# A triangular solve by chunk in two 64x64 blocks per head, in one core's hybrid decoder layer

## The reference, cut to what matters

```python
decay = jnp.exp(jnp.where(tri, gam[..., :, None] - gam[..., None, :], -jnp.inf))
kb = kc * bc[..., None]
M = jnp.tril(jnp.einsum('nbhrd,nbhsd->nbhrs', kb, kc) * decay, -1)
A = M + jnp.eye(L, dtype=M.dtype)
rhs = jnp.concatenate([vc * bc[..., None], kb * jnp.exp(gam)[..., None]], axis=-1)
X = lax.linalg.triangular_solve(A, rhs, left_side=True, lower=True, unit_diagonal=True)
U, W = X[..., :dv], X[..., dv:]
```

## Time and profile before

| | us |
|---|---|
| median of 3 runs (lowest, highest) | 1853.58 (1852.49, 1855.44) |
| the profiled execution | 1853.64 |
| its span, from the first to the last instruction | 1851.8 |
| PE busy | 1829.1 (99%) |
| PEld busy | 1582.3 (85%) |
| DVE busy | 1065.3 (58%) |
| ACT busy | 855.7 (46%) |
| POOL busy | 452.2 (24%) |

### The profile page before, as it was taken

How to read it: one execution, slowest core, us unless ns; L and a number is a source line. 1 busy time by engine, 2 the same in 40 slices (tenths; PEclk the granted TensorE clock), 3 DMA queues, 4 the chain that set the end, 5 groups by cost and what they waited for, 6 DMA issues and landing times.

```text
span 1851.8 us, 26888 instructions
## 1 busy us (share of the span) xinstructions
PE 1829.1 (99%) x10213; PEld 1582.3 (85%) x10213; DVE 1065.3 (58%) x1267; ACT 855.7 (46%) x1004; POOL 452.2 (24%) x242
## 2 busy tenths in 40 slices
PE   8999999999999999999999999999999999999997
PEld 6888988888888888888888878888888888888886
DVE  5677743455655675555555356666666666543334
ACT  5555445435643344444444354444444444444444
POOL 5222533112231122222222232222222222222223
PEclk9999999999999999999999999999999999999999
DMA  7566443444444456656667636665566566655553
GB/s 209 168 182 192 138 126 125 121 130 137 159 157 128 137 184 196 189 182 189 191 187 248 200 130 193 192 189 186 182 192 188 185 192 188 211 193 192 193 193 135
DMA packets 263432, 324.50 MB, mean 175 GB/s; under 512 B 16779, under 2 KB 230213, under 8 KB 262725
## 3 DMA queue, kind: packets, MB, share of 16 engines
q1 hardware_dynamic: 263366, 323.58, 55.3%
HBM read 321.45 MB, written 2.10 MB: 175 GB/s over the span
## 4 chain that ended last, share of the span: by engine, by line
PE 96%; DVE 2%; ACT 1%; issue 0%; DMA 0%; DVEq 0%; SPq 0%; ACTq 0%
PE ps L571 94%; PE ps L652 0%; DVE xs L1799 0%; PE ps L722 0%; DMA x_in<-in_x_dram 0%; ACT p L992 0%; DVE w_lo L380 0%; PE ps L683 0%; PE ps L870 0%; ACT w_hi L375 0%; ACT L992 0%; PE ps L847 0%; DVE gvt L1667 0%; DVE p L1434 0%; DVE fmax L1439 0%
## 5 line engine op out<-in xcount | busy, mean ns | idle before, releaser
L375 ACT ACTIVATE w_hi<-raw 128x1024 fp32r<-128x1024 f32 x601 | 635.0, 1059 | 872.5 <-PE ps L571 861.2
L380 DVE TENSOR_TENSOR w_lo<-raw,w_hi 128x1024 fp32r<-128x1024 f32 x450 | 561.9, 1255 | 504.1 <-ACT w_hi L375 503.4
L571 PE MATMUL ps<-xnT,w_hi 128*128 128x512 f32 (+1 forms) x2960 | 750.2, 395 | 0.9 <-issue 0.8
L380 POOL TENSOR_TENSOR w_lo<-raw,w_hi 128x1024 fp32r<-128x1024 f32 x151 | 368.2, 2438 | 1307.8 <-ACT w_hi L375 1307.7
L571 PEld LDWEIGHTS ps<-xnT,w_hi 128*128 128x128 f32 (+1 forms) x2960 | 532.4, 189 | 99.1 <-issue 1.5
L571 PEld LDWEIGHTS ps<-xnT,w_lo 128*128 128x128 f32 (+1 forms) x2960 | 404.2, 190 | 29.3
L571 PE MATMUL ps<-xnT,w_lo 128*128 128x256 f32 (+1 forms) x2960 | 415.4, 282 | 0.0
L571 PE MATMUL ps<-w_hi,xnT 128*128 128x512 f32 x1408 | 356.6, 392 | 0.0
L571 PEld LDWEIGHTS ps<-w_hi,xnT 128*128 128x128 f32 x1408 | 261.3, 188 | 52.8 <-issue 0.2
L571 PE MATMUL ps<-w_lo,xnT 128*128 128x512 f32 x704 | 192.4, 390 | 1.6 <-DVE w_lo L380 1.6
L571 PEld LDWEIGHTS ps<-w_lo,xnT 128*128 128x128 f32 x704 | 132.0, 188 | 29.8 <-DVE w_lo L380 2.3
(11 more groups left out here) (330 smaller groups left out, 1089.7 us busy)
## 6 DMA issues: line engine op xcount, KB each, us to landing
raw<-in_w_in_dram SPq DMA_DIRECT2D x256, 512.0 KB, 3.6
raw<-in_w_up_dram SPq DMA_DIRECT2D x176, 512.0 KB, 3.6
raw<-in_w_down_dram SPq DMA_DIRECT2D x88, 512.0 KB, 4.6
raw<-in_w_out_dram SPq DMA_DIRECT2D x32, 512.0 KB, 4.7
raw<-in_w_fox_proj_dram SPq DMA_DIRECT2D x16, 512.0 KB, 4.1
raw<-in_w_gdn_proj_dram SPq DMA_DIRECT2D x16, 512.0 KB, 3.2
raw<-in_w_ml_proj_dram SPq DMA_DIRECT2D x16, 512.0 KB, 3.8
x_in<-in_x_dram SPq DMA_DIRECT2D x4, 512.0 KB, 5.7
```

The source lines that it names most:

```text
L375: act.activation(w_hi[:, s, 0:n], raw[:, s, 0:n], ACT.Copy).then_inc(hi_ready[s], 1)
L380: eng.tensor_tensor(w_lo[:, s, 0:n], raw[:, s, 0:n], w_hi[:, s, 0:n], ALU.subtract).then_inc(lo_ready[s], 1)
L571: return pe.matmul(o, l, r, start=start, stop=stop)
```

## The change

Both chunks of a tile are now kept one above the other, as blocks of 64 columns: nt_, nlv, xm and xmt become [128, NT, H, 64], with chunk 0 in partitions 0 to 63 and chunk 1 in 64 to 127. Each product of 128x128 becomes two of 64x64, one with rows and columns 0 to 63 of the array and one with 64 to 127, issued in turn for each head. The two write different partitions of the same bank.

- **plan_items**: all items of both tiles for one step share a slot, and steps are two slots apart. Steps: solve_p 0, solve_p 1, then for levels 1 to 5 solve_x and solve_p; 24 items in 12 slots, 64, 66 to 86. wt is at 88 instead of 96. What follows moves 8 slots earlier, from dc on 6. mturn gets a bound on the chunks of mlqk, and dc one more slot behind mlv, with a wait for each.
- **solve_p** of level lv > 0 first transposes xm (16 products with the identity, into the pair's second bank) and then, but for the last (6), multiplies nlv by xm (16, into the first bank). Level 0 multiplies nlv by the identity. ACT copies the transpose to xmt; DVE scales the product by c_m into the new tile xp, at level 0 also forms xm, and then waits for ACT's copy (xt_turned) before it frees the pair. solve_xt is gone.
- **solve_x** (levels 1 to 5): xmt times xp, 16 products; DVE subtracts it from xm.
- **wt** and **u**: 16 products instead of 8, each of one block; wt writes a bank for each block.
- **DVE** forms nt_ in two operations of 64 partitions; its block of six operations (kbg, gvt, gkt) comes behind solve_p of level 5.
- **POOL**: masks of 128x512 instead of 128x1024; the two triangular selects on nt_ (L1936) are gone, one addition folds the level masks, one makes ident_c.

```diff
+    out += [(at, "solve_p", (tt, 0)) for tt in range(NT)]
+    at += 2
     for lv in range(LEVELS):
-        row = [("solve_p", 0), ("solve_p", 1)]
-        row += [("solve_x", 0), ("solve_x", 1)] * (0 < lv < LEVELS - 1)
-        row += [("solve_xt", 0), ("solve_xt", 1)]
-        for name, tt in row:
-            out.append((at, name, (tt, lv)))
-            at += 1
+        for name in ("solve_x",) * (0 < lv < LEVELS) + ("solve_p",):
+            out += [(at, name, (tt, lv + (name == "solve_p"))) for tt in range(NT)]
+            at += 2
...
-    out.append((gx, "mturn", ()))
+    out.append((max(gx, last_chunk("mlqk", 3) + 2), "mturn", ()))
...
-    at = max(at, last_chunk("mlv", 1)) + 1
+    at = max(at, last_chunk("mlv", 1) + 1) + 1
...
+        BLOCKS = (slice(0, L), slice(L, P))
+
+        def within(ap, b):
+
+            return ap[:, b, :].rearrange("p (h l) -> p h l", l=L)
...
                 elif name == "solve_p":
                     tt, lv = args
-                    pe.wait_ge(S["level_ready"], 2 * lv + tt + 1)
+                    if lv < LEVELS:
+                        pe.wait_ge(S["level_ready"], 2 * lv + tt + 1)
...
-                    for h in range(H):
-                        if lv:
-                            last = mm(oh[:, h, :], nlv[:, tt, h, :], xm[:, tt, h, :])
-                        else:
-                            last = pe.transpose(oh[:, h, :], nlv[:, tt, h, :], ident[:, :])
+                    for h in range(H * (lv > 0)):
+                        for r in BLOCKS:
+                            last = mm(within(o, 1)[r, h, :], xm[r, tt, h, :], ident[r, r])
+                    for h in range(H * (lv < LEVELS)):
+                        for r in BLOCKS:
+                            last = mm(within(o, 0)[r, h, :], nlv[r, tt, h, :], xm[r, tt, h, :] if lv else ident[r, r])
                 elif name == "solve_x":
                     tt, lv = args
                     item_read(pe, "solve_p", tt, lv)
...
+                        for r in BLOCKS:
+                            last = mm(within(o, 0)[r, h, :], xmt[r, tt, h, :], xp[r, tt, h, :])
...
-                        last = mm(oh[:, h, :], kbg[:, tt, h, :], xmt[:, tt, h, :])
...
+                        for cb, r in enumerate(BLOCKS):
+                            last = mm(within(o, cb)[:, h, :], kbg[r, tt, h, :], xmt[r, tt, h, :])
...
-                        last = mm(oh[:, h, :], xmt[:, tt, h, :], gvt[:, tt, h, :])
...
+                        for r in BLOCKS:
+                            last = mm(oh[r, h, :], xmt[r, tt, h, :], gvt[r, tt, h, :])
...
-                    for h in range(H):
-                        last = f(pm_[:, tt, h, :], heads(o)[:, h, :], ACT.Identity, scale=c_m[:, tt, h:h + 1], bias=0.0)
-                    last.then_inc(free, 1)
...
+                    f(xmt[:, tt, :, :], within(o, 1), ACT.Copy).then_inc(S["xt_turned"] if lv < LEVELS else free, 1)
...
+                    tt_(xp[:, tt, :, :], within(o, 0), over_free(c_m[:, tt, :], L), ALU.mult).then_inc(S["xp_ready"], 1)
+                    dve.wait_ge(S["xp_ready"], 2 * lv + tt + 1)
+                    if lv == 0:
+                        dve.wait_ge(S["ident_ready"], 1)
+                        tt_(xm[:, tt, :, :], over_heads(ident_c[:, :], H), xp[:, tt, :, :],
                             ALU.subtract).then_inc(S["x_start"], 1)
+                    else:
+                        dve.wait_ge(S["xt_turned"], 2 * (lv - 1) + tt + 1)
+                    dve.sem_inc(free, 1)
+                elif name == "solve_x":
+                    tt, lv = args
+                    item_written(dve, k)
+                    if lv == 1:
+                        dve.wait_ge(S["x_start"], tt + 1)
+                    tt_(xm[:, tt, :, :], xm[:, tt, :, :], within(o, 0), ALU.subtract).then_inc(free, 1)
```

More of the change, by code:

```diff
@@ L245, in hybrid_layer_kernel @@
         start_b = small("start_b", [P, NT])
+        ident_c = small("ident_c", [P, L])
         arena = cursor[0] + (-cursor[0]) % 1024
@@ L266, in hybrid_layer_kernel @@
         aqk = part("aqk", 8, [P, NT, H, P])
-        nt_ = part("nt", 10, [P, NT, H, P])
-        xm = part("xm", 12, [P, NT, H, P])
-        xmt = part("xmt", 14, [P, NT, H, P])
+        nt_ = part("nt", 10, [P, NT, H, L])
+        xmt = part("xmt", 14, [P, NT, H, L])
         pm_ = part("pm", 16, [P, NT, H, P])
+        xp = part("xp", 16, [P, NT, H, L])
+        xm = part("xm", 17, [P, NT, H, L])
         ed = part("ed", 18, [P, NT, H, P])
         sq = part("sq", 18, [P, NT, H, HD])
-        nlv = part("nlv", 18, [P, NT, H, P])
+        nlv = part("nlv", 18, [P, NT, H, L])
         st = part("st", 10, [P, H, HD])
@@ L707, in item @@
                     item_read(pe, "solve_p", tt, lv)
-                    if lv:
-                        item_read(pe, "solve_xt", tt, lv - 1)
                     for h in range(H):
[L711 to L717, removed]
-                    for h in range(H):
[L719 to L722, removed]
+                        for r in BLOCKS:
+                            last = mm(within(o, 0)[r, h, :], xmt[r, tt, h, :], xp[r, tt, h, :])
                 elif name == "wt":
@@ L725, in item @@
                     pe.wait_ge(S["kbg_ready"], tt + 1)
-                    item_read(pe, "solve_xt", tt, LEVELS - 1)
+                    item_read(pe, "solve_p", tt, LEVELS)
                     for h in range(H):
-                        last = mm(oh[:, h, :], kbg[:, tt, h, :], xmt[:, tt, h, :])
+                        for cb, r in enumerate(BLOCKS):
+                            last = mm(within(o, cb)[:, h, :], kbg[r, tt, h, :], xmt[r, tt, h, :])
                 elif name == "u":
@@ L1036, in item @@
                     f(ed[:, tt, :, :], ed[:, tt, :, :], ACT.Exp).then_inc(S["e_exp"], 1)
-                elif name == "solve_p":
+                elif name == "solve_p" and args[1] > 0:
                     tt, lv = args
                     item_written(act, k)
[L1040 to L1043, removed]
-                        last = f(pm_[:, tt, h, :], heads(o)[:, h, :], ACT.Identity, scale=c_m[:, tt, h:h + 1], bias=0.0)
-                    last.then_inc(free, 1)
-                elif name == "solve_xt" and 0 < args[1] < LEVELS - 1:
-                    item_written(act, k)
-                    f(xmt[:, args[0], :, :], heads(o), ACT.Copy).then_inc(free, 1)
+                    f(xmt[:, tt, :, :], within(o, 1), ACT.Copy).then_inc(S["xt_turned"] if lv < LEVELS else free, 1)
                 elif name == "wt":
@@ L1051, in item @@
                     item_written(act, k)
-                    f(wq[:, tt, :, 0:4:3, :], heads(o).rearrange("p h (b l) -> p h b l", l=L), ACT.Copy,
+                    f(wq[:, tt, :, 0:4:3, :], o.rearrange("p b (h l) -> p h b l", l=L), ACT.Copy,
                       scale=-1.0).then_inc(free, 1)
@@ L1370, in item @@
                     dve.wait_ge(S["dk_ready"], tt + 1)
-                    tt_(nt_[:, tt, :, :], oh, ed[:, tt, :, :], ALU.mult).then_inc(free, 1)
+                    for r in BLOCKS:
+                        last = tt_(nt_[r, tt, :, :], oh[r, :, r], ed[r, tt, :, r], ALU.mult)
+                    last.then_inc(free, 1)
                 elif name == "qk":
@@ L1381, in item @@
                     tt_(q_t, q_t, pm_[:, tt, :, :], ALU.mult).then_inc(S["qg_ready"], 1)
-                elif name == "solve_x" or name == "solve_xt" and args[1] in (0, LEVELS - 1):
+                elif name == "solve_p" and args[1] < LEVELS:
                     tt, lv = args
                     item_written(dve, k)
-                    m = (xm if name == "solve_x" else xmt)[:, tt, :, :]
-                    tt_(m, m if lv else over_heads(ident[:, :], H), oh, ALU.subtract).then_inc(free, 1)
                     if lv == 0:
-                        tt_(xm[:, tt, :, :], over_heads(ident[:, :], H), pm_[:, tt, :, :],
-                            ALU.subtract).then_inc(S["x_start"], 1)
+                        dve.wait_ge(S["qg_ready"], 2)
+                        dve.wait_ge(S["coef_ready"], 1)
+                    tt_(xp[:, tt, :, :], within(o, 0), over_free(c_m[:, tt, :], L), ALU.mult).then_inc(S["xp_ready"], 1)
[3 more added lines that the diff above has]
+                        tt_(xm[:, tt, :, :], over_heads(ident_c[:, :], H), xp[:, tt, :, :],
+                            ALU.subtract).then_inc(S["x_start"], 1)
+                    else:
[7 more added lines that the diff above has]
+                    tt_(xm[:, tt, :, :], xm[:, tt, :, :], within(o, 0), ALU.subtract).then_inc(free, 1)
                 elif name == "ws":
@@ L1717, in _ @@
                     item(k)
-                    if ITEMS[k][1] == "solve_xt" and ITEMS[k][2] == (1, LEVELS - 1):
+                    if ITEMS[k][1] == "solve_p" and ITEMS[k][2] == (1, LEVELS - 1):
                         for tt in range(NT):
@@ L1914, in _ @@
                 keep(v, ALU.is_ge, -b, [[0, n], [1, 2 * b]], 0)
```

(4 more changed lines are left out.)

8 lines of the change are left out of this document (4 added, 4 removed).

## The result

The changed kernel takes 1840.35 us (median of 6 runs, 1838.13 to 1844.64) against 1852.59 us for the kernel before (6 runs, 1850.62 to 1855.44). The medians differ by 12.2 us. The ratio on record is 0.9938, 95% interval 0.9928 to 0.9948, which makes 11.5 us, from 9.6 to 13.3. Timed again later it was 0.9935 (0.9921 to 0.9948). The forecast was 9.3 us less than the profiled execution of before, 1844.3 us. The profiled execution of the changed kernel took 1840.31 us, its span is 1838.6 us. Two executions, 2116.16 us for the kernel before (timed beside the experiments) and 4646.22 us for the version with two banks, were slow ones and count in no figure.

What follows compares the result with a forecast made beforehand. TensorE (PE) was taken as the bound, 96% of the last chain. -46.4 + 32.6 + 4.6 + (7.0 + 1.5 - 7.2) - 1.4 = -9.3 us from 1853.64 gives 1844.3 us; own range 1839.5 to 1850, with rivals to 1866.

Steps and rivals of the forecast that it cites:

- The price of a small product: PE, new solve: a 64x64x64 product takes 0.06 us as two row halves overlap; range 0.055 to 0.12.
- New solve: PE, the solve: 544 small products at 0.06 us, 32.6 us, plus 4.6 us of shape changes; old solve 46.4 us.
- Turns of shape: PE, solve slots: going into a 64-row shape and back costs 0.38 us, once a slot, 4.6 us for 12.
- wt and u: PE, wt and u items: 7.2 us before, 7.0 us after plus 1.5 us of shape changes.
- The wait at level 1: PE before its first nlv product: the 1.4 us wait for VectorE's late xm goes; bound 0.5 us lost.
- 3.3 us to either side: Clock behind dc: the two falls there may come, go or double as items move, 3.3 us either way.
- 1 (no overlap, 1880 us): PE, small products: halves writing the same bank wait for one another, 0.12 us a product, kernel 1880.5 us; chance 0.13.
- 2 (feeding): PE, new solve: four instructions a product come only every 0.10 us, kernel +12.5, 1866 us; chance 0.12.
- 3: PE, small products: halves partly overlap, 0.07 to 0.09 us each, -3.9 to +7.0, about 1855 us; chance 0.17.
- 4 (falls of the clock in the solve): Five solve_p slots: each brings a clock fall of 1.7 us, 8.3 us together, kernel 1852.6 us; chance 0.08.

Runs made afterwards that it cites:

- the version with two banks: The changed kernel, but solve_x writes the two halves' products to separate banks and VectorE subtracts them in two operations; 1839.84 us, ratio 0.9935 to the kernel before.
- the experiment with grouped halves: The changed kernel, but each solve item issues all lower-half products, then all upper-half ones, not in turn; 1864.11 us, ratio 1.0060 to the kernel before.
- the one-item slots: The changed kernel with the two tiles' solve items in neighbouring slots, 24 slots instead of 12; 1845.28 us, ratio 0.9965 to the kernel before.
- the first version in quarters: The changed kernel, but odd heads use the array's other two quarters in solve_x and solve_p at levels 1 to 5; 1828.70 us, ratio 0.9862.
- the version with wt in quarters: The four-quarter kernel with wt cut into quarters, wt and u items paired, VectorE's six-operation block moved behind solve_x of level 5; 1826.08 us, ratio 0.9861.
- the kernel before in pairs: The kernel before, its 128x128 solve items unchanged, but both tiles' items of a step in one slot; 1849.71 us, ratio 0.9991.

## Why the prediction was right

**The price of a small product** carried the forecast. It was built from two rows that were neither of them the operation: dc for the cost of one half alone (0.12), mqk for the sharing by two halves (one half). 0.06 was forecast, 0.058 measured, and the experiment with grouped halves showed both parts: 0.117 us within one half, half of it in turn. One reading in it was a judgement: mqk's 1.10 us for 8 products are 0.14 each with the turn in them, and 0.11 only if some 0.2 us are set aside for the turn. At 0.14 the price would have come out at some 0.07. wt of the changed kernel bears the 0.11 out: (2.15 - 0.35)/16 = 0.11. New solve: 37.2 forecast with the turns, 35.8 measured. The stretch from the first solve item to the first wt, 104 us by forecast, took 324.32 - 221.92 = 102.4.

**Turns of shape.** 0.38 us forecast from ds, 0.35 from the changed kernel's slots and again from the one-item slots. 12 more are saved by sharing.

**wt and u.** +1.3 forecast, +1.4 measured. That nothing would be gained there, as either the loads or the moving data have 128 columns, held; for wt the quarters showed that it is the loads.

**The wait at level 1.** All of the 1.4 us was booked as gained. VectorE's timeline at level 0 of the changed kernel:

```profile
226.71 1.18 DVE L1388 TENSOR_TENSOR xm<-ident_c,xp 128x512 f32<-128x512 f32 x1
...
228.52 0.69 DVE L1388 TENSOR_TENSOR xm<-ident_c,xp 128x512 f32<-128x512 f32 x1
```

The first xm is there at 227.9, PE asks for it at 229.72: 1.8 us to spare, where 1.5 were forecast. Two operations were slow beside GpSimd all the same, a w_lo before these (1.76 us from 223.18, others 1.22) and the first xm (1.18 us, the second 0.69). GpSimd's masks take 1.6 us each where they took 2.9; that this is why xm is no longer late is likely, but no run isolates it.

**Sum.** -10.6 + 1.4 - 1.4 = -10.6 us by the slots, -9.3 forecast, -11.5 (9.6 to 13.3) measured. The 1840.35 us lie near the lower end of the forecast's own range, 1839.5 to 1850.

**The rest of the profiled pair.** Its spans differ by 13.2 us, 2.6 more than the slots. The windows of the clock (us, busy PE, PEld, DVE, ACT, POOL with counts, clock, DMA share, GB/s), first two of the changed kernel:

```profile
400.00:600.00 200.00, 198.60 (x1176) 166.41 (x1175) 117.11 (x161) 90.82 (x118) 44.14 (x27) 1.00 0.49 145
...
1090.82:1097.65 6.83, 5.31 (x19) 3.95 (x20) 6.83 (x8) 4.96 (x8) 3.03 (x2) 0.50 0.15 51
```

and one of the kernel before:

```profile
1102.04:1112.28 10.24, 7.78 (x25) 5.84 (x26) 10.24 (x11) 6.32 (x9) 3.94 (x3) 0.50 0.28 93
```

Before had two falls of the clock behind dc (the earlier trace rows has the first), worth 1.7 us each; after has none. Around the norm before the MLP, where PE waits for VectorE and GpSimd, before had 10.24 us at half clock and after 6.83; between the w_lo groups on either side that is 1.1 us less. Against that, PE of the changed kernel was 2.4 us behind within the first 26 us, and so its first solve item begins late (221.92 against 219.46). 3.4 + 1.1 - 2.4 is 2.1 of the 2.6 us; 0.2 is the w_lo wait of 1.6 us in exchange for one of 1.4 on mkt, and the rest is left open.

No run shows that any of the three belongs to the change. The changed kernel was profiled a second time, and two of them went the other way: 10.24 us at half clock around the norm, as before had, and its first solve item at 219.99; its span is 1838.0 us. The falls behind dc it had in neither profile. But they come and go between executions of one kernel: the first version in quarters had two in its first profile and none in its second, and so had the version with wt in quarters. One item per slot and two banks had none, the kernel before in pairs and the grouped halves one. So of the 11.5 us the mechanism accounts for 10.6, and that the rest fell on the same side was, as far as the runs show, luck. The forecast had left it at 3.3 us to either side.

**The rivals.** 1 (no overlap, 1880 us) fell: 5.00 us for the solve_x slot and not 6.9, with the same bank and with two. The Trainium skill's rule in "TensorEngine Tiling (Array Packing)", section "Restrictions and Gotchas", that different row tiles cannot access the same PSUM bank at once, would have given that rival; the runs differ from it, and they decide: row halves that write different partitions of one bank took 0.058 us a product, as they did with two banks. 2 (feeding) fell with the quarters at 0.029. 3 fell with 0.058. 4 (falls of the clock in the solve) didn't happen: the granted clock stayed at full speed (1.00) from 220 to 330 us.

**What was off** is a size: 0.06 rounds up 0.058, and with 544 products that and 0.38 for 0.35 is the 1.4 us between 37.2 and 35.8. In the experiments the one clear miss was the grouped order, 22 to 24 us instead of 32, for the overlap at the seams.

## What to carry to other kernels

When PE is the bound, cost a change of shape by starts in the stream, and ask of small products how many quarters of the array neighbours in the order use: 0.117 us in one, 0.058 in two, 0.029 in four, for the same float32 product of 64x64x64, and only if neighbours alternate. Keep products of one shape together, since each way out of the full shape and back costs 0.35 us. And cutting products into more but smaller ones can pay even when the instructions become 2.6 times as many (832 loads and multiplications for the solve before, 2176 after).

## What the hardware showed that was not expected

- Loads and multiplications of four quarters overlap fully: 16 instructions for four products in 4 x 0.029 = 0.12 us, what one product takes in one quarter.
- With the halves grouped, PE still ran products of both at once around a change of half, also across the seam of two items (231.96 and 232.01 in the timeline; 3.18 us for 32 products, where 3.74 would be without any overlap).
- Two row halves write one bank at once at no cost when their partitions differ (5.00 us with one bank, 5.00 with two).
- The granted clock fell to 0.50 behind dc in some executions of a kernel and not in others: two falls of 3.41 us and none in two profiles of the first version in quarters.
